# The last FFN product with token tiles stationary: two transformer layers in fp32 on one NeuronCore

## The chip, the cores and the metric

One core of a Trainium2 chip runs one launch of the kernel. The metric is the device time of that launch in microseconds (us), as the median of the runs; lower is better. Sequence length is 256, model width 2048, all inputs and outputs are fp32.

## The reference, cut to what matters

Two layers: multi-head latent attention and a convolutional FFN, then sliding-window attention and a second FFN, then a final norm. The change touches what follows the second FFN's gate:

```python
def _rmsnorm(x, g):
    y = xf * lax.rsqrt(jnp.mean(xf * xf, axis=-1, keepdims=True) + EPS)
    return (y * g.astype(F32)).astype(x.dtype)
...
    return (jax.nn.silu(gate) * val) @ w_out        # (256 x 5632) @ (5632 x 2048)
...
        h = h + _conv_ffn(_rmsnorm(h, norm_ffn[i]), ...)
    return _rmsnorm(h, final_norm)
```

## The kernel before, in words

**Weights in chunks.** All weights form one stream of 682 chunks of 128 x 1024 floats (512 KB). For the last product (phase `f1_out`, 88 chunks) a chunk holds two row tiles of 128 rows of `w_out` by 512 columns. Each chunk goes through four slots: SyncE loads it into `raw` (L364), ScalarE copies it to `w_hi` in the reduced format fp32r (`split`, L822), VectorE subtracts to get the rest `w_lo` (`split`, L1103), TensorE uses both. The activation is held in the same two parts, `op_ffn[:, tile, 0, :]` high and `op_ffn[:, tile, 1, :]` low, so that high by high, high by low and low by high give nearly fp32 products.

**The order of work** is written by hand in a block per engine and bound by semaphores. `lo_ready` counts chunks split, `chunk_used` chunks that TensorE has used. ScalarE's split of chunk n waits until chunk n-4 is used; SyncE's load waits for the split of the chunk that had the slot. The engines' other work is put between the splits.

**The last product** (`groups` with `w_chunk`, L419) has 4 groups of 22 chunks. A group makes 512 features for all 256 tokens, features on the partitions. Weights are stationary: for each of 4 feature tiles and 2 row tiles, `feature_tile` (L406) issues `w_hi` against high and low part of the activation side by side (512 moving columns, L409) and `w_lo` against the high part (256 moving columns, L412), so a chunk is 8 + 8 matmuls. In a group's last chunk the second row tile has the two in the other order. A group uses 4 of the 8 PSUM banks, and the groups alternate. VectorE adds the two halves of a bank to the residual `h` (features on partitions) in two passes (L1353, L1360), after the split of the third chunk beyond the group. GpSimd squares `h` of the first three groups and adds up (L1612, L1615). VectorE multiplies their 12 tiles by the final gain (L1377) between splits of the last group.

**The end.** After the last matmul of the last group: VectorE adds the last residual (L1353, L1360), TensorE transposes 16 tiles of 128 x 128 (L789), then 8, then sums squares over partitions with one-column matmuls (L803, L805), ScalarE squares the last 512 features (L1080), loads its table and takes the root (L1082), VectorE inverts it (L1591). TensorE transposes the last 8 tiles. ScalarE (L1088) and VectorE (L1596) scale the transposed tiles out of PSUM into `yt`, and SyncE stores four pieces of 512 KB (L397), each of 128 tokens by 1024 features, each after one pass of both engines.

Phases of attention have two other kinds of product that the prediction draws on: `token_chunk` (L430), where a tile of 128 tokens is stationary and 256 columns of the weights move (L438 to L440), and `narrow_chunk` (L691 to L693), where weights are stationary and 256 columns of the activation move, three times.

## Time and profile before

| | |
|---|---|
| median of 3 runs | 2021.43 us (2020.96 to 2022.01) |
| the profiled execution | 2018.73 us, its span 2016.7 us |
| TensorE busy, matmul | 1984.6 us (98%) |
| TensorE busy, weight load | 1763.1 us (87%) |
| VectorE busy | 1432.0 us (71%) |
| ScalarE busy | 987.3 us (49%) |
| GpSimd busy | 145.2 us (7%) |
| DMA | 374.46 MB, mean 186 GB/s |

The profile is of one execution. Its own time lies 2.0 us above its span, and 2.7 us below the median of the runs. "Busy" counts instructions that execute; matmuls overlap in the pipeline, so the distance from one start to the next says what a matmul costs, and its duration does not. "Idle before" is the time in which an engine waited in front of an instruction, with the releaser.

### The profile page before, as it was taken

The numbers are of one execution on the slowest core, as the hardware profiler recorded it, in microseconds if no ns is written. First come the engines' busy times: TensorE is split into PE (matmuls) and PEld (weight loads), VectorE is DVE, ScalarE is ACT, GpSimd is POOL, SyncE is SP. The second block draws the span as 40 slices with busy tenths as digits, with TensorE's granted clock in tenths as the row PEclk, the third lists the DMA queues.
The fourth block names the chain that finished last, engine by engine and source line by source line (L and its number), as shares of the span: only waits on it lengthen the run. The fifth ranks groups of instructions, "written<-read, shape, count | busy, mean of one in ns | idle before, by whom it ended". The sixth has DMA issues, their size and how long they took to land.

```text
span 2016.7 us, 33814 instructions
## 1 busy us (share of the span) xinstructions
PE 1984.6 (98%) x12008; PEld 1763.1 (87%) x12008; DVE 1432.0 (71%) x1980; ACT 987.3 (49%) x1151; POOL 145.2 (7%) x147
## 2 busy tenths in 40 slices
PE   7899999999999999999999999999999999999998
PEld 6798888888888888888899888888888888888887
DVE  7866777787788777555566668878887887855554
ACT  6456345555554554334445554555455555533332
POOL 1103230000000000110120004100000000001110
PEclk9999999999999999999999999999999999999999
DMA  7457555555555555555565334555556555555553
GB/s 277 151 195 167 178 188 186 199 189 182 198 185 175 196 194 195 185 188 198 188 236 185 126 127 161 199 193 187 177 189 206 188 179 196 186 195 190 189 188 115
DMA packets 103880, 374.46 MB, mean 186 GB/s; under 512 B 11547, under 2 KB 12124, under 8 KB 103548
## 3 DMA queue, kind: packets, MB, share of 16 engines
q1 hardware_dynamic: 101180, 362.55, 53.0%
q0 software_dynamic: 2624, 10.83, 2.1%
q8 instruction: 56, 0.92, 0.2%
q14 instruction: 20, 0.16, 0.0%
HBM read 364.94 MB, written 8.39 MB: 185 GB/s over the span
## 4 chain that ended last, share of the span: by engine, by line
PE 90%; DVE 5%; issue 1%; ACT 0%; DVEq 0%; ACTq 0%
PE ps L409 53%; PE ps L412 28%; PE ps L691 2%; PE ps L693 1%; PE ps L692 1%; DVE w_lo L1103 1%; DVE scores_b L1496 1%; PE ps L729 1%; PE ps L740 1%; PE ps L752 1%; PE ps L440 1%; PE ps L439 1%; PE ps L438 1%; DVE cv L1118 0%; PE ps L621 0%
## 5 line engine op out<-in xcount | busy, mean ns | idle before, releaser
L1103 DVE TENSOR_TENSOR w_lo<-raw,w_hi 128x1024 fp32r<-128x1024 f32 (+1 forms) x682 | 829.9, 1230 | 498.2 <-ACT w_hi L822 476.8
L822 ACT ACTIVATE w_hi<-raw 128x1024 fp32r<-128x1024 f32 (+1 forms) x682 | 715.2, 1055 | 794.6 <-PE ps L412 607.3
L409 PE MATMUL ps<-op_in,w_hi 128*128 128x512 f32 x2992 | 1028.0, 391 | 9.4 <-DVE w_lo L1103 9.4
L412 PE MATMUL ps<-op_in,w_lo 128*128 128x256 f32 x2992 | 812.9, 282 | 0.0
L409 PEld LDWEIGHTS ps<-op_in,w_hi 128*128 128x128 f32 x2992 | 549.6, 188 | 113.7 <-issue 8.3
L412 PEld LDWEIGHTS ps<-op_in,w_lo 128*128 128x128 f32 x2992 | 565.5, 189 | 15.7
L409 PE MATMUL ps<-op_ffn,w_hi 128*128 128x512 f32 x1408 | 486.2, 390 | 0.0
L412 PE MATMUL ps<-op_ffn,w_lo 128*128 128x256 f32 x1408 | 391.7, 282 | 0.0
L409 PEld LDWEIGHTS ps<-op_ffn,w_hi 128*128 128x128 f32 x1408 | 262.2, 188 | 53.0
L412 PEld LDWEIGHTS ps<-op_ffn,w_lo 128*128 128x128 f32 x1408 | 266.0, 189 | 2.7
L1612 POOL TENSOR_TENSOR cg<-h 128x1024 f32 (+1 forms) x15 | 43.1, 2876 | 1604.9 <-DVE h L1360 1454.4
L409 PE MATMUL ps<-op_att,w_hi 128*128 128x512 f32 x384 | 132.3, 392 | 2.7 <-issue 1.5
L412 PE MATMUL ps<-op_att,w_lo 128*128 128x256 f32 x384 | 104.2, 282 | 0.0
L409 PEld LDWEIGHTS ps<-op_att,w_hi 128*128 128x128 f32 x384 | 70.5, 188 | 16.5 <-issue 1.6
L1405 DVE SCALAR_TENSOR_TENSOR cv<-up,par,cv 128x256 f32<-128x256 f32 x176 | 73.6, 480 | 6.5 <-DVE cv L1400 3.4
L1405 DVE SCALAR_TENSOR_TENSOR cg<-up,par,cg 128x256 f32<-128x256 f32 x176 | 73.6, 480 | 6.6 <-DVE cg L1400 3.4
L412 PEld LDWEIGHTS ps<-op_att,w_lo 128*128 128x128 f32 x384 | 72.5, 189 | 1.9
L691 PE MATMUL ps<-op_in,w_hi 128*128 128x256 f32 x256 | 73.5, 287 | 0.0
L692 PE MATMUL ps<-op_in,w_lo 128*128 128x256 f32 x256 | 71.4, 279 | 0.0
L693 PE MATMUL ps<-op_in,w_hi 128*128 128x256 f32 x256 | 71.4, 279 | 0.0
L835 ACT ACTIVATE op_ffn<-cv 128x1024 f32 x22 | 23.4, 1066 | 93.0 <-DVE cv L1430 93.0
L1615 POOL TENSOR_TENSOR sqa<-sqa,cg 128x256 f32<-128x256 f32 x60 | 62.6, 1043 | 4.7
(198 smaller groups left out, 1626.2 us busy)
## 6 DMA issues: line engine op xcount, KB each, us to landing
raw<-weights SPq DMA_DIRECT2D x666, 512.0 KB, 3.8
raw<-weights SPq DMA_DIRECT2D x16, 384.0 KB, 3.1
bias_rows<-brow POOLq DMA_DIRECT2D x1, 6144.0 KB, 36.6
win_bias<-bias_rows POOLq DMA_DIRECT2D x4, 1024.0 KB, 8.4
h<-xt SPq DMA_DIRECT2D x8, 256.0 KB, 8.1
x_tok<-x_rows SPq DMA_DIRECT2D x2, 1024.0 KB, 10.6
y<-yt SPq DMA_DIRECT2D x4, 512.0 KB, 4.0
par<-params SPq DMA_DIRECT2D x1, 352.0 KB, 11.9
```

The source lines that it names most:

```text
L409: return mm(ps[:, bank, 0:2 * T], whi, op, start=start, stop=stop)
L412: return mm(ps[:, bank, 0:T], wlo, op[:, 0, :], start=False, stop=False)
L438: mm(o, hi, wcols(w_hi[s], k), start=first and k == 0, stop=False)
L691: mm(o, w_hi[s][:, w], op[:, kt0 + k, 0, :], start=first and k == 0 and j % 2 == 0, stop=False)
L692: mm(o, w_lo[s][:, w], op[:, kt0 + k, 0, :], start=False, stop=False)
L693: z = mm(o, w_hi[s][:, w], op[:, kt0 + k, 1, :], start=False, stop=last and k == 1 and j % 2 == 1)
L822: f(w_hi[s][:, 0:cols], raw[s][:, 0:cols], ACT.Copy).then_inc(hi_ready, 1)
L835: f(dst, cv[:, :, :], ACT.Copy).then_inc(operand_hi, 1)
L1103: v.tensor_tensor(w_lo[s][:, 0:cols], raw[s][:, 0:cols], w_hi[s][:, 0:cols].bitcast(F32), ALU.subtract).then_inc(lo_ready, 1)
L1405: z = v.scalar_tensor_tensor(dst[:, m, :], up[:, m, tap:T + tap], col(tile0 + (w + tap * CT + m)), dst[:, m, :], ALU.mult, ALU.add)
L1612: done(g_.tensor_tensor(tmp, src, src, ALU.mult))
L1615: z = g_.tensor_tensor(acc[:, :], acc[:, :], tmp[:, j, :], ALU.add)
```

## The change: what it does

- The last product is computed with tokens on the partitions. `rows_chunk` takes 128 tokens of the activation as the stationary operand (high part twice, low part once) and 512 columns of the chunk's weights as the moving one: for 2 token tiles and 2 row tiles `hi` by `w_hi`, `hi` by `w_lo`, `lo` by `w_hi`. That is 12 matmuls of 512 columns for a chunk. A group fills 2 banks.
- `turn_h`: after the ninth chunk of each group TensorE transposes the 8 tiles of the group's part of the old residual into the other 2 banks of the group's four, and ScalarE copies them back over `h`, 4 x 256 columns, which now holds tokens on the partitions.
- VectorE adds product and residual in two passes of 128 x 512 for each group (`add_rows`), multiplies by the gain, now a row (`gain_rows`), into `yt`. ScalarE squares each half and sums along the row (`accum_out`), and takes the root from the sum of the last group with the sum of the other three as bias; it has taken a root of that bias earlier in the last group.
- The rows of `gain_row` (1 MB, one row read for all partitions) come by a DMA of GpSimd after the last chunk of `f1_in`. GpSimd's squares for the final norm are gone; so are the end's transposes and one-column matmuls, and the gains by feature.
- `yt` is scaled in place and stored in eight pieces of 256 KB, 128 tokens by 512 features each.

```diff
...
     ra = region(KT * 2 * T * 4)
     op_in = place("op_in", [P, KT, 2, T], F32R, ra)
     yt = place("yt", [P, 2, D], F32, ra)
+    gain_row = place("gain_row", [P, D], F32, ra + 2 * D * 4)
     probs_t = [place("probs_t0", [P, 2, 384], F32, ra), place("probs_t1", [P, 2, 384], F32, ra + 29312)]
     scores_sb = place("scores_sb", [P, 2, 2, 384], F32, ra + 3072)
...
             rest = PH["a_kv"].c0
             repeat(sp, 0, (CHUNKS - rest) // SLOTS, lambda i: [load(Lin(rest + k, SLOTS, i)) for k in range(SLOTS)])
-            for k in range(4):
-                half, cols = k // 2, slice(k % 2 * (D // 2), (k % 2 + 1) * (D // 2))
-                sp.wait_ge(y_act, k + 1)
-                sp.wait_ge(y_dve, k + 1)
-                sp.dma_start(out[half * P:(half + 1) * P, cols], yt[:, half, cols]).then_inc(stored, 16)
-            sp.wait_ge(stored, 64)
+            for half in range(2):
+                for ready, q in ((y_act, 0), (y_dve, 2), (y_act, 1), (y_dve, 3)):
+                    sp.wait_ge(ready, 2 * half + q % 2 + 1)
+                    cols = slice(q * COLS, (q + 1) * COLS)
+                    sp.dma_start(out[half * P:(half + 1) * P, cols], yt[:, half, cols]).then_inc(stored, 16)
+            sp.wait_ge(stored, 128)
             sp.wait_ge(bias_out, 16)
...
                 for c in range(8):
                     w_chunk(Lin(ph.c0 + 8 * gi + c), op_att, 2 * c, c == 0, c == 7, b0).then_inc(chunk_used, 1)
             groups(PH["f1_in"], op_in, KT, op_wait(OP0["b_out"]), norm=5)
-            groups(PH["f1_out"], op_ffn, FT, op_wait(OP0["f1_in"]))
-
-
-            def transposes(q, src, bank):
-
-                pe.wait_ge(y_scaled, q + 1)
+
+            ph = PH["f1_out"]
+
+            def rows_chunk(n, kt0, first, last, bank):
+
+                s = n % SLOTS
+                pe.wait_ge(lo_ready, n + 1)
                 for half in range(2):
-                    if q == 3 and half == 1:
-                        pe.wait_ge(norm_root_taken, 7)
-                    for j in range(4):
-                        z = nc.tensor.transpose(ps[:, bank + half, j * P:(j + 1) * P],
-                                                src(j)[:, half * P:(half + 1) * P], ident[:, :])
-                    z.then_inc(y_transposed, 1)
-            yb = OUT_BANKS
-            pe.wait_ge(banks_free, PH["f1_out"].g1 - 1)
-            transposes(0, lambda j: h[:, j, :], yb[0])
-            transposes(1, lambda j: h[:, 4 + j, :], yb[1])
-            pe.wait_ge(banks_free, PH["f1_out"].g1)
-            transposes(2, lambda j: h[:, 8 + j, :], yb[2])
-            pe.wait_ge(squares_added, NORM_SQ[6])
-            pe.wait_ge(last_squares, 1)
-            for half in range(2):
-                tokens = slice(half * P, (half + 1) * P)
-                o = ps[:, yb[3] + 1, half:half + 1]
-                mm(o, sqa[:, tokens], ones[:, 0:1], start=True, stop=False)
+                    t = slice(half * P, (half + 1) * P)
+                    for k in range(2):
+                        w = slice(k * COLS, (k + 1) * COLS)
+                        hi, lo = op_ffn[:, kt0 + k, 0, t], op_ffn[:, kt0 + k, 1, t]
+                        mm(ps[:, bank + half, :], hi, w_hi[s][:, w], start=first and k == 0, stop=False)
+                        mm(ps[:, bank + half, :], hi, w_lo[s][:, w], start=False, stop=False)
+                        z = mm(ps[:, bank + half, :], lo, w_hi[s][:, w], start=False, stop=last and k == 1)
+                z.then_inc(chunk_used, 1)
+
+            def turn_h(g, bank):
+
+                if g >= 2:
+                    pe.wait_ge(h_turned, g - 1)
                 for j in range(4):
-                    z = mm(o, cg[:, j, tokens], ones[:, 0:1], start=False, stop=j == 3)
-            z.then_inc(norm_sum, 1)
-            transposes(3, lambda j: cv[:, j, :], yb[3])
+                    for half in range(2):
+                        at = j % 2 * T + half * P
+                        z = nc.tensor.transpose(ps[:, bank + j // 2, at:at + P],
+                                                h[:, 4 * g + j, half * P:(half + 1) * P], ident[:, :])
+                z.then_inc(h_transposed, 1)
+            for g in range(4):
+                b0 = 4 * (g % 2)
+                if g < 2:
+                    pe.wait_ge(banks_free, ph.g0 + g - 1)
+                else:
+                    pe.wait_ge(y_summed, 2 * (g - 1))
+                for c in range(FT // 2):
+                    if g == 0 and c % 2 == 0:
+                        pe.wait_ge(operand_lo, OP0["f1_in"] + c // 2 + 1)
+                    rows_chunk(ph.c0 + FT // 2 * g + c, 2 * c, c == 0, c == FT // 2 - 1, b0)
+                    if c == 8:
+                        turn_h(g, b0 + 2)
         @block.scalar
...
             residual(PH["b_out"], KT, OP0["b_out"], second=True)
             norm_root(5, inv_rms[:, :], 4 - 4 * (PH["f1_in"].g0 % 2), D)
             ffn_in(PH["f1_in"], 1, OP0["f1_in"])
-            residual(PH["f1_out"], FT, None)
-
-
-            act.wait_ge(banks_free, PH["f1_out"].g1)
-            f(cg[:, :, :], h[:, KT - 4:KT, :], ACT.Square).then_inc(last_squares, 1)
-            act.wait_ge(norm_sum, 7)
-            f(rs_col[:, 4:6], ps[:, OUT_BANKS[3] + 1, 0:2], ACT.Sqrt, bias=eps[:, 0:1],
-              scale=1.0 / D).then_inc(norm_root_taken, 1)
-            act.wait_ge(sqrt_done, 1)
+
+            ph = PH["f1_out"]
+
+            def quads(bank):
+
+                a = ps[:, bank, 0:T]
+                return bass.AP(a.tensor, a.offset, [list(a.ap[0]), [T, 4], [1, T]])
+            for g in range(4):
+                for c in range(FT // 2):
+                    split(Lin(ph.c0 + AHEAD + FT // 2 * g + c))
+                    if c == 6:
+                        act.wait_ge(h_transposed, g + 1)
+                        f(h[:, 4 * g:4 * g + 4, :], quads(4 * (g % 2) + 2), ACT.Copy).then_inc(h_turned, 1)
+                    if c == 19:
+                        for half in range(2):
+                            act.wait_ge(y_summed, 2 * g + half + 1)
+                            f(cg[:, 0:4, half * P:(half + 1) * P], h[:, 4 * g:4 * g + 4, half * P:(half + 1) * P],
+                              ACT.Square, scale=D ** -0.5,
+                              accum_out=y_sums[:, g, half:half + 1]).then_inc(y_squared, 1)
+                            if g == 3:
+                                act.wait_ge(y_squared, 7 + half)
+                                f(y_rs[:, half:half + 1], y_sums[:, 3, half:half + 1], ACT.Sqrt,
+                                  bias=y_rest[:, half:half + 1]).then_inc(norm_root_taken, 1)
+                    if g == 3 and c == 4:
+                        act.wait_ge(y_rest_ready, 1)
+                        f(y_rs[:, :], y_rest[:, :], ACT.Sqrt)
             for half in range(2):
-                for q in (0, 2):
-                    act.wait_ge(y_transposed, 2 * q + half + 1)
-                    f(yt[:, half, q * 512:(q + 1) * 512], ps[:, OUT_BANKS[q] + half, :], ACT.Copy,
-                      scale=rs_col[:, 4 + half:5 + half]).then_inc(y_act, 1)
+                act.wait_ge(y_rs_ready, half + 1)
+                for q in range(2):
+                    cols = slice(q * COLS, (q + 1) * COLS)
+                    f(yt[:, half, cols], yt[:, half, cols], ACT.Copy, scale=y_rs[:, half:half + 1]).then_inc(y_act, 1)
         @block.vector
...
             inverse(5, [inv_rms[:, :]])
             dve.wait_ge(operand_lo, OP0["b_out"] + 4)
             ffn_in(PH["f1_in"], 1, OP0["f1_in"])
-            residual(PH["f1_out"], FT, None, None, static=True)
-
-
-            for m in range(4):
-                z = v.tensor_scalar(cv[:, m, :], h[:, KT - 4 + m, :], col(Lin(PC_FIN + KT - 4 + m)), None, ALU.mult)
-            z.then_inc(y_scaled, 1)
-            dve.wait_ge(norm_root_taken, 7)
-            v.reciprocal(rs_col[:, 4:6], rs_col[:, 4:6]).then_inc(sqrt_done, 1)
-            dve.wait_ge(sqrt_done, 1)
+
+            ph = PH["f1_out"]
+
+            def rows(g, half):
+                return h[:, 4 * g:4 * g + 4, half * P:(half + 1) * P]
+
+            def add_rows(g, half):
+
+                o = ps[:, 4 * (g % 2) + half, :].rearrange("p (m t) -> p m t", m=4)
+                v.tensor_tensor(rows(g, half), o, rows(g, half), ALU.add).then_inc(y_summed, 1)
+
+            def gain_rows(g, half):
+
+                cols = slice(g * COLS, (g + 1) * COLS)
+                dve.wait_ge(y_summed, 2 * g + half + 1)
+                v.tensor_tensor(yt[:, half, cols].rearrange("p (m t) -> p m t", m=4), rows(g, half),
+                                gain_row[:, cols].rearrange("p (m t) -> p m t", m=4), ALU.mult).then_inc(y_gained, 1)
+
+            def inverse_rms(half):
+
+                dve.wait_ge(norm_root_taken, 7 + half)
+                v.reciprocal(y_rs[:, half:half + 1], y_rs[:, half:half + 1]).then_inc(y_rs_ready, 1)
+            for g in range(4):
+                for c in range(FT // 2):
+                    split(Lin(ph.c0 + AHEAD + FT // 2 * g + c))
+                    if c == 17:
+                        dve.wait_ge(h_turned, g + 1)
+                        dve.wait_ge(chunk_used, ph.c0 + FT // 2 * (g + 1))
+                        add_rows(g, 0)
+                        add_rows(g, 1)
+                    if c == 19 and g < 3:
+                        if g == 0:
+                            dve.wait_ge(gain_row_in, 16)
+                        gain_rows(g, 0)
+                        gain_rows(g, 1)
+                    if g == 3 and c == 2:
+                        dve.wait_ge(y_squared, 6)
+                        done(v.tensor_tensor(y_rest[:, :], y_sums[:, 0, :], y_sums[:, 1, :], ALU.add))
+                        done.sync()
+                        done(v.tensor_tensor(y_rest[:, :], y_rest[:, :], y_sums[:, 2, :], ALU.add))
+                        done.sync()
+                        v.tensor_scalar(y_rest[:, :], y_rest[:, :], EPS, None, ALU.add).then_inc(y_rest_ready, 1)
+            gain_rows(3, 0)
+            inverse_rms(0)
+            gain_rows(3, 1)
+            inverse_rms(1)
+            dve.wait_ge(y_gained, 8)
             for half in range(2):
-                for q in (1, 3):
-                    dve.wait_ge(y_transposed, 2 * q + half + 1)
-                    v.tensor_scalar(yt[:, half, q * 512:(q + 1) * 512], ps[:, OUT_BANKS[q] + half, :],
-                                    rs_col[:, 4 + half:5 + half], None, ALU.mult).then_inc(y_dve, 1)
+                dve.wait_ge(y_rs_ready, half + 1)
+                for q in range(2, 4):
+                    cols = slice(q * COLS, (q + 1) * COLS)
+                    v.tensor_scalar(yt[:, half, cols], yt[:, half, cols], y_rs[:, half:half + 1], None,
+                                    ALU.mult).then_inc(y_dve, 1)
         @block.gpsimd
...
                 heads = bass.AP(bias_dram.tensor, P - 1 + 8 * k * P * 384, [[383, P], [P * 384, 8], [1, T]])
                 pool.dma_start(win_bias[:, 8 * k:8 * k + 8, :], heads).then_inc(win_bias_in[k], 16)
             residual_squares(PH["b_out"], SQ0["b_out"])
-            pool.wait_ge(norm_sum, 6)
-            done(g_.memset(sqa[:, :], 0.0))
-            done.sync()
-            for gi in range(3):
-                pool.wait_ge(banks_free, PH["f1_out"].g0 + gi + 1)
-                squares(h[:, 4 * gi:4 * gi + 4, :], cg[:, :, :], sqa, None)
-                pool.wait_ge(squares_added, SQ0["f1_out"] + gi + 1)
+            pool.wait_ge(chunk_used, PH["f1_in"].c1)
+            pool.dma_start(gain_row[:, :], bass.AP(final_gain.tensor, 0, [[0, P], [1, D]])).then_inc(gain_row_in, 16)
 def tables():
```

TensorE in the last product before, where one chunk ends and the next begins (all chunks of a group but its last look so). The names are PSUM, then the moving operand, then the stationary one.

```order
L412 MATMUL ps<-op_ffn,w_lo_58 128x256
L409 MATMUL ps<-op_ffn,w_hi_54 128x512
L412 MATMUL ps<-op_ffn,w_lo_58 128x256
L409 MATMUL ps<-op_ffn,w_hi_55 128x512 [waits lo_ready]
L412 MATMUL ps<-op_ffn,w_lo_59 128x256
```

A pair of 512 and 256 columns alternates, eight times for each chunk, with one wait at a chunk's start. The same place of the second group now, around the transposes (`ident` moves, a tile of `h` is stationary):

```order
L798 MATMUL ps<-w_hi_53,op_ffn 128x512
L796 MATMUL ps<-w_hi_53,op_ffn 128x512
L797 MATMUL ps<-w_lo_57,op_ffn 128x512
L798 MATMUL ps<-w_hi_53,op_ffn 128x512
L808 MATMUL ps<-ident,h 128x128 x8
L796 MATMUL ps<-w_hi_54,op_ffn 128x512 [waits lo_ready]
L797 MATMUL ps<-w_lo_58,op_ffn 128x512
L798 MATMUL ps<-w_hi_54,op_ffn 128x512
```

All matmuls have 512 columns, and the eight transposes wait for nothing here (in the third and fourth group the first of them waits for `h_turned`).

VectorE's program after its last split, before:

```order
L1353 TENSOR_TENSOR h<-h,ps 128x1024 [waits banks_free,chunk_used]
L1360 TENSOR_TENSOR h<-h,ps 128x1024 [waits dve_done]
L1588 TENSOR_SCALAR cv<-h,par 128x256 [waits banks_free]
L1588 TENSOR_SCALAR cv<-h,par 128x256 x3
L1591 RECIPROCAL rs_col<-rs_col 128x2 [waits norm_root_taken]
L1596 TENSOR_SCALAR yt<-ps,rs_col 128x512 [waits y_transposed,sqrt_done]
L1596 TENSOR_SCALAR yt<-ps,rs_col 128x512 [waits y_transposed] x3
```

and now:

```order
L1612 TENSOR_TENSOR h<-ps,h 128x4x128 [waits chunk_used,h_turned]
L1612 TENSOR_TENSOR h<-ps,h 128x4x128
L1618 TENSOR_TENSOR yt<-h,gain_row 128x512 [waits y_summed]
L1624 RECIPROCAL y_rs<-y_rs 128x1 [waits norm_root_taken]
L1618 TENSOR_TENSOR yt<-h,gain_row 128x512 [waits y_summed]
L1624 RECIPROCAL y_rs<-y_rs 128x1 [waits norm_root_taken]
L1654 TENSOR_SCALAR yt<-yt,y_rs 128x512 [waits y_rs_ready,y_gained]
```

The passes are half as wide, nothing waits for TensorE after the first row, and each half of the tokens has its own root. ScalarE's end, now:

```order
L1104 ACTIVATE cg,y_sums<-h 128x4x128 [waits y_summed]
L1109 ACTIVATE y_rs<-y_sums,y_rest 128x1 [waits y_squared]
L1104 ACTIVATE cg,y_sums<-h 128x4x128 [waits y_summed]
L1109 ACTIVATE y_rs<-y_sums,y_rest 128x1 [waits y_squared]
L1118 ACTIVATE yt<-yt,y_rs 128x512 [waits y_rs_ready]
```

Both roots stand ahead of the first scaled copy, and no table is loaded there.

## Rows read from the trace of the kernel before

**Rows 1.** The page: granted clock by slice, and the chain's shares by engine.

```profile
PEclk9999999999999999999999999999999999999999
...
PE 90%; DVE 5%; issue 1%; ACT 0%; DVEq 0%; ACTq 0%
```

**Rows 2.** Waits, 1758 to 2001 us: who waited for whom, us, times, longest.

```profile
ACT w_hi L822 <- PE ps L412: 132.7, 78, 2.0
DVE w_lo L1103 <- ACT w_hi L822: 107.1, 76, 1.8
```

**Rows 3.** Timeline, ScalarE: start us, us, engine, line, out<-in, [idle before <-releaser].

```profile
1824.20 1.06 ACT L822 ACTIVATE w_hi<-raw 128x1024 fp32r<-128x1024 f32 x1 [1.71 <-PE ps L412]
...
1871.34 1.06 ACT L822 ACTIVATE w_hi<-raw 128x1024 fp32r<-128x1024 f32 x1 [1.71 <-PE ps L412]
```

**Rows 4.** Timeline, TensorE, last chunk of the last group (order turned round).

```profile
1998.92 0.40 PE L412 MATMUL ps<-op_ffn,w_lo 128*128 128x256 f32 x2
...
2001.01 0.40 PE L412 MATMUL ps<-op_ffn,w_lo 128*128 128x256 f32 x2
2001.25 0.39 PE L409 MATMUL ps<-op_ffn,w_hi 128*128 128x512 f32 x1
```

**Rows 5.** Timeline, TensorE, 256 columns of the activation moving.

```profile
1042.35 0.28 PE L691 MATMUL ps<-op_in,w_hi 128*128 128x256 f32 x1
...
1055.65 0.28 PE L691 MATMUL ps<-op_in,w_hi 128*128 128x256 f32 x1
```

**Rows 6.** Timeline, TensorE, 256 columns of the weights moving.

```profile
1038.11 0.28 PE L438 MATMUL ps<-w_hi,op_in 128*128 128x256 f32 x1
...
1039.53 0.39 PE L409 MATMUL ps<-op_in,w_hi 128*128 128x512 f32 x1
```

**Rows 7.** Timeline, ScalarE: splits released by a group's last matmul.

```profile
1291.20 1.06 ACT L822 ACTIVATE w_hi<-raw 128x1024 fp32r<-128x1024 f32 x1 [1.71 <-PE ps L409]
...
1757.54 1.06 ACT L822 ACTIVATE w_hi<-raw 128x1024 fp32r<-128x1024 f32 x1 [1.72 <-PE ps L409]
```

**Rows 8.** Timeline, TensorE, six transposes among an attention phase's matmuls.

```profile
1097.40 0.28 PE L693 MATMUL ps<-op_in,w_hi 128*128 128x256 f32 x1
1097.82 0.84 PE L740 MATMUL ps<-ident,probs_b 128*128 128x128 f32 x6
1098.42 0.37 PE L691 MATMUL ps<-op_in,w_hi 128*128 128x256 f32 x1
1098.62 0.28 PE L692 MATMUL ps<-op_in,w_lo 128*128 128x256 f32 x1
```

**Rows 9.** Timeline, all engines, the end.

```profile
2001.48 1.91 PE L789 MATMUL ps<-ident,h 128*128 128x128 f32 x16
2001.68 1.22 DVE L1353 TENSOR_TENSOR h<-h,ps 128x1024 f32<-128x1024 f32 x1 [8.72 <-PE ps L409]
...
2004.19 1.06 ACT L1080 ACTIVATE cg<-h 128x1024 f32<-128x1024 f32 x1 [12.49 <-DVE h L1360]
...
2007.79 0.26 ACT L1082 ACTIVATE rs_col<-ps,eps 128x2 f32<-128x2 f32 x1 [1.25 <-PE ps L805]
...
2009.14 2.95 SPq L397 DMA_DIRECT2D y<-yt  x4
```

**Rows 10.** Groups by line and shape: xcount | busy us, mean ns | idle before.

```profile
L1246 DVE TENSOR_TENSOR q_nope<-ps,half_b 128x512 f32<-128x512 f32 x4 | 2.7, 685 | 0.0
...
L1088 ACT ACTIVATE yt<-ps,rs_col 128x512 f32<-128x512 f32 x4 | 2.4, 688 | 0.2 <-PE ps L789 0.2
...
L789 PE MATMUL ps<-ident,h 128*128 128x128 f32 x24 | 3.0, 275 | 0.8 <-DVE h L1360 0.8
```

**Rows 11.** DMA: packets of 2010 to 2015 us (the stores), then of the first 20 us.

```profile
DMA packets 539, 2.02 MB, mean 403 GB/s; under 512 B 48, under 2 KB 48, under 8 KB 538
...
DMA packets 2471, 6.53 MB, mean 327 GB/s; under 512 B 265, under 2 KB 521, under 8 KB 2347
```

**Rows 12.** Waits, 1042 to 1056 us, with 1 MB loads of GpSimd under way.

```profile
ACT w_hi L822 <- DMA raw<-weights: 3.6, 2, 1.9
```

More of the change, by code:

```diff
@@ L95, in attention_banks @@
     return scores, 4 - scores, 6 - scores
-OUT_BANKS = [(4 * (PH["f1_out"].g1 % 2) + 2 * k) % 8 for k in range(4)]
 class Lin:
@@ L343, in build @@
         outputs_lo = sem("outputs_lo")
-        y_scaled = sem("y_scaled")
-        last_squares = sem("last_squares")
-        y_transposed = sem("y_transposed")
+        gain_row_in = sem("gain_row_in")
+        h_transposed = sem("h_transposed")
+        h_turned = sem("h_turned")
+        y_summed = sem("y_summed")
+        y_squared = sem("y_squared")
+        y_gained = sem("y_gained")
+        y_rs_ready = sem("y_rs_ready")
+        y_rest_ready = sem("y_rest_ready")
         y_act = sem("y_act")
@@ L981, in residual @@
                     body(None, 1)
-                elif k0 is not None:
+                else:
                     repeat(act, 0, 2, body)
-                else:
-                    body(None, 0)
-                    body(None, 1)
             def ffn_in(ph, layer, k0):
@@ L1389, in residual @@
                     body(None, 1)
-                elif static:
-                    for t in range(turns):
-                        body(None, t)
                 else:
```

19 lines of the change are left out of this document (8 added, 11 removed).

## The prediction

> **What bounds the kernel now.** I read the page first: the chain that ended last is 90% TensorE, and the granted clock is at its upper level, 2.4 GHz, in every slice [rows 1]. Then the waits of the last product's stretch: ScalarE waits for TensorE 78 times, VectorE for ScalarE 76 times, and no row has TensorE waiting [rows 2]. So in this stretch a weight chunk costs what TensorE takes to issue its matmuls. From 1824.20 to 1871.34 us there are 17 chunks, 47.14 / 17 = 2.773 us each [rows 3]; 88 chunks make 244.0 us. Behind the last matmul the end is a chain through all engines: VectorE starts at 2001.68, the first store is issued at 2009.14 [rows 9], and the span ends at 2016.7. That is 7.46 us to the first store, 7.6 us from there, and 15.05 us in all. A faster matmul stream and a shorter end both count in full; all that hides behind TensorE counts nothing.
>
> All sums are against the profiled execution, 2018.73 us. The median of the runs lies 2.7 us above it, and I add that at the end. A measurement can tell about 0.2% (4 us) from no change.
>
> **Term 1, the matmuls.** Removed are 16 a chunk, 8 of 512 and 8 of 256 moving columns, added are 12 of 512: 6144 columns either way. The question is what a 512-column matmul costs when only such follow each other, and when weights move. A pair of 512 and 256 now costs 2.773 / 8 = 0.3466 us. Alone, 256 columns of the activation cost (1055.65 - 1042.35) / 38 / 3 = 0.1167 us [rows 5], which leaves 0.2299 for the 512. The last chunk of a group has 512 behind 512: from 1998.92 to 2001.01 there are three sets of two and two, 0.6967 each [rows 4]. Less one pair, that is 0.3501 for one 256 behind a 256 and one 512 behind a 512. With 0.40 - 0.28 = 0.12 for the first of these [rows 4] the 512 costs 0.230, with 0.1167 it costs 0.2334. I take the middle, 0.232, which also leaves something for the weights as moving operand: 12 matmuls with 256 columns of weights took 1039.53 - 1038.11 = 1.42 us, 0.1183 each [rows 6] against 0.1167. A chunk is then 12 x 0.232 = 2.784 us, 0.011 more than now, and 88 of them cost **+1.0 us**.
>
> The bounds. Most: 21 groups of 8 chunks took 1757.54 - 1291.20 = 466.34 us [rows 7], 22.207 each, or 0.023 above 8 x 2.773. If all of that is the four 512-behind-512 of a group's end, each costs 0.2299 + 0.0058 = 0.2357, and +4.9 us in all. Least: a 256 behind another is 0.12 in rows 4 and 0.1167 in a long run of them [rows 5], so equal neighbours may get cheaper in a run; the same 0.0033 off 0.2301 leaves 0.2268, and -4.5 us. One nanosecond per matmul is 1.06 us here, and nothing else in the sum weighs as much.
>
> **Term 2, the transposes in the stream.** Each group now has 8. Six of them among the attention's matmuls start at 1097.82 and the next matmul starts at 1098.42, 0.100 each, and that one costs 0.20 instead of 0.117, so 0.083 for the change back [rows 8]. The 16 behind the last product took 1.91 - 0.27 = 1.64 us for 15 steps, 0.109 each [rows 9], where 0.27 is the length of one [rows 10]. So a group pays 8 x 0.109 + 0.08 = 0.95 us, four pay **+3.8 us**. At least it is 4 x 0.8 = 3.2. At most the gap ahead of the six also counts, 0.42 - 0.12 = 0.30 us [rows 8], which makes 5.0; but the 16 started 0.23 us behind the last 512-column matmul [rows 4, 9], with no such gap. Of the waits for `h_turned` in groups 2 and 3, ScalarE's copy is two groups old, so I cost them at nothing.
>
> What that transposing feeds costs nothing either: ScalarE's copy of 1024 columns (about the 1.06 of its split) and VectorE's passes for three groups go into the idle time of engines that wait 1.7 us in each chunk of 2.77 [rows 3]. The adds stand where the old ones stood. If this cover were gone, each us would go straight to TensorE through `lo_ready`.
>
> **Term 3, the end.** Counted from VectorE's start, 0.43 us behind the last matmul's start [rows 4, 9], which I keep. One add of 128x512: 0.69 [rows 10]. ScalarE's square of half the tokens: 0.65, between half of L1080's 1.06 [rows 9] and the 0.69 of a pass of 512 out of PSUM [rows 10], and 0.10 for reading the sum, an estimate of mine below the root's 0.26, the smallest pass of ScalarE in the rows. Together 0.75. Root 0.26 [rows 9]. The second square and root come before the first scaled copy: another 1.01. The copy 0.69 [rows 10]. Sum 0.69 + 0.75 + 0.26 + 1.01 + 0.69 = 3.40, with four handovers of 0.035 (2004.19 is 2.51 behind 2001.68, with two passes of 1.22 between [rows 9]) 3.55 us to the first store, instead of 7.46. VectorE meanwhile needs four passes of 0.69, 2.8, and two reciprocals of two columns, and is not late. What is late next is the DMA. The stores are 2.10 MB at 403 GB/s, 5.2 us [rows 11], out of the 7.6 behind the first issue, and smaller pieces do not shorten that: a piece of 256 KB takes 0.65 us, and two engines finish one each 0.3. So 3.55 + 7.6 = 11.15 instead of 15.05, **-3.9 us**. Bounds: pieces with rows of 2 KB may go at the 327 GB/s of the mixed loads at the start [rows 11], 1.2 us more, and a late copy may add 0.4: -2.3. Squares at half of L1080, 0.53 without a tail: -4.3, rounded to -4.5.
>
> **Term 4, edits that cost nothing.** The 1 MB of gains lands beside the first chunks. In the attention phase such loads made ScalarE wait 3.6 us for `raw` [rows 12], while VectorE and TensorE went on. GpSimd's squares and VectorE's gains were behind TensorE and give nothing back.
>
> **Sum.** 1.0 + 3.8 - 3.9 = +0.9 us: 2019.6 for a profiled execution, **2022.3 us** as a median. The extremes are -4.5 + 3.2 - 4.5 = -5.8 and +4.9 + 5.0 - 2.3 = +7.6. The work that leaves the end goes into the stream at nearly the same price.
>
> **Rivals.**
> - *Cheaper matmuls (faster).* With a fixed 10 ns beside the columns, as at 256 (0.1167 against 256 / 2.4 GHz = 0.1067), a 512 costs 0.2233, a chunk 2.680, and the total is -8.2 + 3.8 - 3.9 = -8.3: 2013.1. For it: fewer instructions and weight loads. Against: the pairs leave 0.2299. Chance 0.09. A further step is a matmul at its bare columns, 512 / 2.4 GHz = 0.2133: 12 of them make 2.560, the term is -18.7 and the total -18.8, 2002.6. No row here comes near it. Chance 0.03.
>  The Trainium skill ("TensorE: Matmul & The Clock Gate", section "Wait — 56ns, not 53.3ns?") gives 215.7 ns from start to start at 512 columns once warm, close to that last case; by it the term would be -16.1 us. The trace disagrees, with 0.2299 in the pairs.
> - *Weights moving are dear (slower).* At 0.2357 for each matmul of L796 to L798, from the groups' ends, the total is +4.9 + 3.8 - 3.9 = +4.8: 2026.2. It decides above 0.2350. For it: rows 6, where moving weights cost 1.6 ns more, which may double at 512. Against: the group's end may hold its own wait. Chance 0.14.
> - *Each transpose costs its length (slower).* At 0.275 us each [rows 10] the 32 would cost 8.8 + 0.3, and the total is 1.0 + 9.1 - 3.9 = +6.2: 2027.6. Against: 16 of them took 1.91 us [rows 9]. Chance 0.04.
>  The Trainium skill (same page, "Part 4: PE-mode transpose") has about 275 ns for one in a kernel, and speaks against this change; the trace has that as the length, 0.27, and 0.109 as the distance.
> - *The end does not get shorter as said:* the stores bound it from the first issue, and with -2.3 instead of -3.9 the total is +2.5, 2023.9, still no change that can be told. It is part of my case.
>
> **How the numbers follow.** My case, all terms within their bounds and the total within 4 us: 0.67, centre 2022.3, its own range 2018.5 to 2025.4. Faster: 0.12 from the matmuls and 0.02 from all bounds falling low, 0.14. Slower: 0.14 + 0.04 + 0.01 for a wait that I have not seen, 0.19. The range reaches down to about the lower extreme, 2016.0, and up to the dear cases, 2027.5; outside are the fast matmuls and the far end of the transposes.
>
> **What would show it.** ScalarE's splits 2.784 us apart in the last product (2.68 or 2.83 for two rivals); 8 transposes within 0.95 us, with no idle of TensorE ahead of them; first store 3.5 us behind VectorE's add, and the span's end 11.2 behind it; no TensorE waits from 1758 on. If VectorE or ScalarE is named as releaser of TensorE there, or `raw` in the first ten chunks, my cover is wrong.

## The result, and the profile after

| | before | after |
|---|---|---|
| median of 20 runs, us | 2021.1 (2018.15 to 2022.84) | 2025.3 (2022.48 to 2026.21) |
| ratio, 95% interval | | 1.0019 [1.0013, 1.0026] |
| profiled execution, us | 2018.73, span 2016.7 | 2025.74, span 2023.9 |

One run of 2179.81 us, at a granted clock of 0.849, is left out of the range and of the ratio; the other 19 have a median of 2025.0. The change makes the kernel some 4 us slower, just under the 0.2% from which a difference counts here; the forecast was +0.9 us, 2022.3.

The page of the kernel after: busy times, granted clock in 40 slices of 50 us, the chain's shares by engine.

```profile
PE 1987.8 (98%) x11636; PEld 1738.0 (86%) x11636; DVE 1423.3 (70%) x1976; ACT 995.7 (49%) x1172; POOL 122.7 (6%) x132
PEclk9999999999999999999999999999999999999999
PE 92%; DVE 3%; issue 1%; ACT 0%; ACTq 0%; DVEq 0%
```

The waits of the changed product, 1758 to 2024 us (who waited for whom: us, times, longest).

```profile
ACT w_hi L837 <- PE ps L798: 132.8, 81, 2.6
DVE w_lo L1132 <- ACT w_hi L837: 122.9, 82, 2.5
ACT cg L1104 <- DVE h L1612: 10.9, 1, 10.9
DVE h L1612 <- PE ps L798: 8.9, 1, 8.9
```

As in [rows 2], TensorE waits for nobody there. One group's transposes, in the timelines of ScalarE (first four rows) and of TensorE: start us, us, engine, line, operation, out<-in, [idle before <-releaser].

```profile
1847.69 1.06 ACT L837 ACTIVATE w_hi<-raw 128x1024 fp32r<-128x1024 f32 x1 [1.74 <-PE ps L798]
1850.48 1.06 ACT L837 ACTIVATE w_hi<-raw 128x1024 fp32r<-128x1024 f32 x1 [1.73 <-PE ps L798]
1854.16 1.06 ACT L837 ACTIVATE w_hi<-raw 128x1024 fp32r<-128x1024 f32 x1 [2.62 <-PE ps L798]
1856.96 1.06 ACT L837 ACTIVATE w_hi<-raw 128x1024 fp32r<-128x1024 f32 x1 [1.74 <-PE ps L798]
...
1849.99 0.39 PE L798 MATMUL ps<-w_hi,op_ffn 128*128 128x512 f32 x1
1850.22 1.04 PE L808 MATMUL ps<-ident,h 128*128 128x128 f32 x8
1851.02 0.48 PE L796 MATMUL ps<-w_hi,op_ffn 128*128 128x512 f32 x1
1851.34 0.40 PE L797 MATMUL ps<-w_lo,op_ffn 128*128 128x512 f32 x1
1851.57 0.40 PE L798 MATMUL ps<-w_hi,op_ffn 128*128 128x512 f32 x1
...
1857.17 0.40 PE L798 MATMUL ps<-w_hi,op_ffn 128*128 128x512 f32 x1
```

A chunk takes 2.80 us (1856.96 less 1854.16) instead of 2.773 [rows 3], and from 1851.57 to 1857.17 there are 24 matmuls of 512 columns, 0.2333 each. The chunk with the transposes takes 3.68, 0.88 more: the eight lie 0.100 apart (1851.02 less 1850.22), and the first matmul behind them takes 0.32 instead of 0.233.

The end, where [rows 9] was, as the timeline has it: the last matmul, the passes of VectorE and ScalarE, the stores.

```profile
2012.21 0.40 PE L798 MATMUL ps<-w_hi,op_ffn 128*128 128x512 f32 x1
2012.72 1.29 DVE L1612 TENSOR_TENSOR h<-ps,h 128x512 f32<-128x512 f32 x2 [8.89 <-PE ps L798]
2013.44 0.63 ACT L1104 ACTIVATE cg<-h 128x512 f32<-128x512 f32 x1 [10.87 <-DVE h L1612]
2013.98 0.19 ACT L1104 ACTIVATION_READ_ACCUMULATOR cg<-h 128x1 f32 x1
2014.20 0.29 ACT L1109 ACTIVATE y_rs<-y_sums,y_rest 128x1 f32<-128x1 f32 x1
2014.40 0.61 ACT L1104 ACTIVATE cg<-h 128x512 f32<-128x512 f32 x1
2015.14 0.29 ACT L1109 ACTIVATE y_rs<-y_sums,y_rest 128x1 f32<-128x1 f32 x1
2015.34 2.54 ACT L1118 ACTIVATE yt<-yt,y_rs 128x512 f32<-128x512 f32 x4
2015.56 1.67 DVE L1654 TENSOR_SCALAR yt<-yt,y_rs 128x512 f32<-128x512 f32 x4
2016.07 4.48 SPq L402 DMA_DIRECT2D y<-yt  x8
```

The first store is issued 3.35 us behind VectorE's start instead of 7.46, and the span's end, 2023.9, is 11.69 us behind the start of the last matmul instead of 15.45 (2016.7 less 2001.25, [rows 4]).

**Where the difference lies.** I cut both records at one mark: ScalarE's split beside the last group end of the product before the last. It is at 1757.54 before [rows 7], and in the timeline of after at:

```profile
1295.99 1.06 ACT L837 ACTIVATE w_hi<-raw 128x1024 fp32r<-128x1024 f32 x1 [1.74 <-PE ps L414]
...
1762.75 1.06 ACT L837 ACTIVATE w_hi<-raw 128x1024 fp32r<-128x1024 f32 x1 [1.74 <-PE ps L414]
```

| stretch, us | before | after | difference |
|---|---|---|---|
| start to the mark | 1757.54 | 1762.75 | +5.2 |
| mark to the last matmul's start | 243.71 | 249.46 | +5.75 |
| last matmul's start to the span's end | 15.45 | 11.69 | -3.76 |

What I had costed, the last two rows, comes to +2.0 us. The other 5.2 us arise before the first instruction that the change was meant to touch. The same two rows of after show a part of it: 21 groups in 466.76 us, 22.227 each, where [rows 7] have 22.207. So the experiments had two tasks: the split of the +2.0, and the cause of the rest.

### The profile page after: what moved, and what is told of

It is laid out like the page before. It is cut to its first block, busy times and chain, and to the rows that moved or that the text cites. A ratio compares the mean times of both kernels' runs of the same rounds, so it can differ in the third digit from the quotient of the medians.

```text
span 2023.9 us, 33059 instructions
## 1 busy us (share of the span) xinstructions
PE 1987.8 (98%) x11636; PEld 1738.0 (86%) x11636; DVE 1423.3 (70%) x1976; ACT 995.7 (49%) x1172; POOL 122.7 (6%) x132
## 4 chain that ended last, share of the span: by engine, by line
PE 92%; DVE 3%; issue 1%; ACT 0%; ACTq 0%; DVEq 0%
PE ps L414 46%; PE ps L417 23%; PE ps L798 4%; PE ps L797 4%; PE ps L796 4%; PE ps L696 2%; PE ps L697 2%; PE ps L698 2%; DVE w_lo L1132 1%; PE ps L734 1%; PE ps L745 1%; PE ps L757 1%; PE ps L444 1%; PE ps L443 1%; PE ps L445 1%
## 5 line engine op out<-in xcount | busy, mean ns | idle before, releaser
L417 PE MATMUL ps<-op_in,w_lo 128*128 128x256 f32 x2992 | 807.4, 280 | 0.0
L414 PE MATMUL ps<-op_ffn,w_hi 128*128 128x512 f32 x704 | 243.2, 392 | 0.0
L417 PE MATMUL ps<-op_ffn,w_lo 128*128 128x256 f32 x704 | 194.2, 280 | 0.0
L414 PEld LDWEIGHTS ps<-op_ffn,w_hi 128*128 128x128 f32 x704 | 131.1, 188 | 27.9
L798 PE MATMUL ps<-w_hi,op_ffn 128*128 128x512 f32 x352 | 140.4, 399 | 0.0
L797 PE MATMUL ps<-w_lo,op_ffn 128*128 128x512 f32 x352 | 138.7, 394 | 0.0
L796 PE MATMUL ps<-w_hi,op_ffn 128*128 128x512 f32 x352 | 138.4, 393 | 0.0
L417 PEld LDWEIGHTS ps<-op_ffn,w_lo 128*128 128x128 f32 x704 | 132.2, 188 | 1.4
L1670 POOL TENSOR_TENSOR cg<-h 128x1024 f32 x12 | 34.6, 2880 | 960.0 <-DVE h L1389 808.8
L797 PEld LDWEIGHTS ps<-w_lo,op_ffn 128*128 128x128 f32 x352 | 66.1, 188 | 17.0
L796 PEld LDWEIGHTS ps<-w_hi,op_ffn 128*128 128x128 f32 x352 | 66.1, 188 | 15.5
L798 PEld LDWEIGHTS ps<-w_hi,op_ffn 128*128 128x128 f32 x352 | 66.1, 188 | 15.3
```

The source lines that it names most:

```text
L414: return mm(ps[:, bank, 0:2 * T], whi, op, start=start, stop=stop)
L417: return mm(ps[:, bank, 0:T], wlo, op[:, 0, :], start=False, stop=False)
L796: mm(ps[:, bank + half, :], hi, w_hi[s][:, w], start=first and k == 0, stop=False)
L797: mm(ps[:, bank + half, :], hi, w_lo[s][:, w], start=False, stop=False)
L798: z = mm(ps[:, bank + half, :], lo, w_hi[s][:, w], start=False, stop=last and k == 1)
L1670: done(g_.tensor_tensor(tmp, src, src, ALU.mult))
```

## The experiments

### Three small tensors: put into the kernel before, and taken out of the new one

The change also adds `y_sums`, `y_rest` and `y_rs`, 32 bytes a partition each. The region with `op_in` and `op_ffn` comes behind them, and its start is rounded up to a multiple of 128 bytes plus 32; 96 bytes more push it 128 bytes up.

```diff
+    pad = new("pad", [P, 24])
     exp_sums = new(...)
```

> The kernel before with 96 bytes of unused SBUF where the change puts its three small tensors, so that all later tiles (op_in, op_ffn among them) lie 128 bytes higher, as in the changed kernel. Theory A (the addresses cost): the splits behind a group of f1_in come 22.227 us apart as in the changed kernel, not 22.207 as before, and the time is 2 us above before (ratio 1.001). Theory B (it was the execution, not the program): 22.207 and a ratio of 1.000.

And the new kernel with the three tensors laid over `sinkc`, which is not needed by then:

```diff
-    y_sums = new("y_sums", [P, 4, 2])
-    y_rest = new("y_rest", [P, 2])
-    y_rs = new("y_rs", [P, 2])
-    sinkc = new("sinkc", [P, HEADS_B])
+    r_sinkc = region(HEADS_B * 4)
+    sinkc = place("sinkc", [P, HEADS_B], F32, r_sinkc)
+    y_sums = place("y_sums", [P, 4, 2], F32, r_sinkc)
+    y_rest = place("y_rest", [P, 2], F32, r_sinkc + 32)
+    y_rs = place("y_rs", [P, 2], F32, r_sinkc + 64)
```

> The changed kernel with its three small tensors laid over sinkc, which is dead by then, so that nothing else moves. Theory A: 22.207 us between the groups of f1_in, ratio to before 1.001 (the 2.0 us that the last product and the end cost together). Theory B: as the changed kernel, 1.002.

The pad alone: 2023.4 us (11 runs) against 2020.66 (27), ratio 1.0017 [1.0008, 1.0026]. The new kernel without the shift: 2022.2 (11 runs), 1.0011 [1.0002, 1.0020]. (The ratios here are those on record; the quotients of the medians, 1.0014 and 1.0008, lie within the intervals.) The two marks in the timeline of the padded kernel, then of the new one without the shift:

```profile
1293.95 1.06 ACT L823 ACTIVATE w_hi<-raw 128x1024 fp32r<-128x1024 f32 x1 [1.74 <-PE ps L410]
1760.71 1.06 ACT L823 ACTIVATE w_hi<-raw 128x1024 fp32r<-128x1024 f32 x1 [1.74 <-PE ps L410]
```

```profile
1290.86 1.06 ACT L838 ACTIVATE w_hi<-raw 128x1024 fp32r<-128x1024 f32 x1 [1.72 <-PE ps L415]
1757.19 1.06 ACT L838 ACTIVATE w_hi<-raw 128x1024 fp32r<-128x1024 f32 x1 [1.72 <-PE ps L415]
```

That is 466.76 us with the pad, to the digit what the new kernel takes, and 466.33 without the shift, against 466.34 before. 96 bytes that nobody reads cost the kernel some 3 us, and only the addresses of the tensors behind them can do it: the instructions are the same. Within a group the chunks keep their 2.77; what grows is the last one, from 2.78 to 2.80 (1762.75 is 2.80 behind the split before it). From the mark on the kernel without the shift takes 249.46 us to the last matmul, the same as the new one, so the local +2.0 does not depend on it.

The groups are not the whole of it. From ScalarE's split at about 64 us on, the padded kernel falls behind the kernel before by 0.38 us up to the group end at 219.38, by 0.58 more up to 1019.12, by 1.16 up to 1246.40, and by 0.46 up to the mark, 2.58 in all. The largest part lies in the stretch with the second attention: 227.28 us before and 227.30 without the shift, 228.44 with the pad and 228.46 in a second record of the new kernel. No run here says why.

### Without the transposes

```diff
-                    if c == 8:
-                        turn_h(g, b0 + 2)
...
-                    if c == 6:
-                        act.wait_ge(h_transposed, g + 1)
-                        f(h[:, 4 * g:4 * g + 4, :], quads(...), ACT.Copy).then_inc(h_turned, 1)
...
-                        dve.wait_ge(h_turned, g + 1)
```

> The changed kernel without the 32 transposes of the residual and without ScalarE's four copies of them, so the residual is added in the wrong layout. Theory (transposes in the stream cost what the trace shows): 3.4 us less than the changed kernel, ratio to before 1.0002. Rival (the transposes fill time that TensorE would lose anyway): less than 1 us gained, ratio 1.0015 or more.

2021.25 us (11 runs), ratio to before 1.0005 [0.9996, 1.0014], which is 2.8 us below the new kernel's 1.0019. The mark is at 1761.66 and the last matmul at 2007.63: 245.97 us, 3.49 less than with the transposes, 0.87 a group. The chunks stay at 2.80. So what is left over the 243.71 of before, 2.26 us, I put down to the matmuls.

### Are the matmuls dear by their addresses?

The region of the weights 32 bytes on, so that `w_hi` lies at 32 of 128 (its address modulo 128) and the operands, unchanged, also at 32:

```diff
+    region(32)
     w_hi = [new(f"w_hi{s}", ...
```

> The changed kernel with w_hi, w_lo and the tiles up to the operands 32 bytes higher, the operand regions where they were. Theory C (512 moving columns of weights cost 0.2333 us for their address, the operands being laid 32 bytes off a multiple of 128): the matmuls of L797 come down to about 0.230, a chunk from 2.80 to 2.76 us, ratio to before 1.0003. Rival D (it is the run of wide matmuls, not the address): 2.80 stays, ratio 1.0019.

Then, from the kernel without the shift, the operands at 64 of 128 with the weights at 0, and both edits together:

```diff
-    top[0] = (top[0] + 127) // 128 * 128 + 32
+    top[0] = (top[0] + 127) // 128 * 128 + 64
```

> As e2_after_noshift, but the operand regions (op_in, op_ffn and what shares them) start 64 bytes beyond a multiple of 128 instead of 32, the weights at a multiple of 128. Only the distances in the trace are read. Theory R (what counts is where stationary and moving operand lie to each other): both kinds of chunk change. Theory M (what counts is where the moving operand lies): the old kind (operand moves) changes from 2.773 us, the new kind (weights move) stays at 2.800. Theory N (addresses below 128 bytes don't matter): both stay.

> Weights 32 bytes and operand regions 64 bytes beyond a multiple of 128, so that the two lie to each other as before. Theory R: old chunks 2.773, new ones 2.800. Theory M: new ones 2.79 as with the weights at 32 and the operands at 32, old ones as in e5_op64. Theory N: fails already on the run with the weights at 32, where old chunks took 2.81.

| weights, operands (address modulo 128) | a group of the old kind, us | mark to last matmul in the new product, us |
|---|---|---|
| 0, 32 (before for the groups; without the shift) | 22.207 | 249.46 |
| 0, 32, operands 128 bytes up (after; pad for the groups) | 22.227 | 249.46 |
| 32, 64 | 22.227 | 249.46 |
| 0, 64 | 22.327 | 249.47 |
| 32, 32 | 22.453 | 248.69 |

The two dearest are means of the last 20 groups. In the row 32, 64 the rounding also puts the operands 128 bytes further up, if the weights of before start at a multiple of 128 as the table has it; it then differs from the second row by 32 bytes on both sides, and has the same times. The times of the whole kernel went the same way: 2038.2 us for weights and operands both at 32 (4 runs, ratio 1.0092 [1.0077, 1.0108]), and in a single run each 2030.8 for 0 and 64, 2024.8 for 32 and 64. In the first of these the old chunks take 2.81 us each; splits of the old kind and then of the new one, in its timeline:

```profile
1314.67 1.07 ACT L838 ACTIVATE w_hi<-raw 128x1024 fp32r<-128x1024 f32 x1 [1.75 <-PE ps L418]
1317.48 1.07 ACT L838 ACTIVATE w_hi<-raw 128x1024 fp32r<-128x1024 f32 x1 [1.74 <-PE ps L418]
...
1896.91 1.06 ACT L838 ACTIVATE w_hi<-raw 128x1024 fp32r<-128x1024 f32 x1 [1.72 <-PE ps L799]
1899.70 1.06 ACT L838 ACTIVATE w_hi<-raw 128x1024 fp32r<-128x1024 f32 x1 [1.73 <-PE ps L799]
```

For the question of the new chunk this was a miss: its 2.80 us hold at four of the five placements and fall only to 2.79 at the fifth (248.69 less 249.46 is 0.77 us over 88 chunks, 0.7 ns a matmul). At the addresses of the new kernel the 512-column matmul costs 0.2333, not the 0.232 that I had taken, and none of these moves is worth more than that 0.7 ns. For the rest of the kernel it was a find: the old kind of chunk is cheapest with a distance of 32 bytes between the residues, dearer with 64, dearest with 0. That is a pattern over five placements, each of which moves other tensors too, and its cause was not looked for.

### The same transposing on VectorE

The kernel without the shift, with the residual turned in blocks of 32x32 by VectorE into `cv`, which is free then: two instructions behind each weight split, 16 steps a group. TensorE's transposes and ScalarE's copies are gone.

```diff
-                        turn_h(g, b0 + 2)
-                        f(h[:, 4 * g:4 * g + 4, :], quads(...), ACT.Copy).then_inc(h_turned, 1)
-                v.tensor_tensor(rows(g, half), o, rows(g, half), ALU.add)
+                v.tensor_tensor(rows(g, half), o, cv[:, 0:4, half * P:(half + 1) * P], ALU.add)
+            def turn_block(g, k):
+                a, b = divmod(k, 4)
+                for half in range(2):
+                    src = h[32 * a:32 * a + 32, 4 * g:4 * g + 4, half * P + 32 * b:half * P + 32 * b + 32]
+                    dst = cv[32 * b:32 * b + 32, 0:4, half * P + 32 * a:half * P + 32 * a + 32]
+                    z = v.transpose(dst, src)
+                z.then_inc(h_turned, 1)
```

> e2_after_noshift with the residual transposed by VectorE instead of TensorE: 16 steps a group, each of two 32 x 512-element blocks of 32x32 transposes that also go to another quarter of the partitions, one step behind each of the first 16 splits; TensorE's 32 transposes and ScalarE's four copies are gone. Theory (VectorE waits 1.5 us in each chunk of 2.8, so steps of about 0.5 us hide): 3.4 us less than e2, ratio to before 0.9993, 1.4 us faster than before. Rival (VectorE becomes late with w_lo, since its steps are far longer than 0.5 us): TensorE waits for VectorE, ratio above 1.001.

2019.4 us (11 runs, 2016.6 to 2021.6) against 2021.1 (21), ratio 0.9989 [0.9980, 0.9998]: the one version that beats both kernels, if by less than the 0.2% that counts here. VectorE in its timeline, and the waits from 1763 to 2015 us:

```profile
1849.85 1.22 DVE L1128 TENSOR_TENSOR w_lo<-raw,w_hi 128x1024 fp32r<-128x1024 f32 x1 [1.05 <-ACT w_hi L836]
1851.11 0.49 DVE L1616 STREAM_TRANSPOSE cv<-h 32x128 f32<-32x128 f32 x2
1852.65 1.22 DVE L1128 TENSOR_TENSOR w_lo<-raw,w_hi 128x1024 fp32r<-128x1024 f32 x1 [1.05 <-ACT w_hi L836]
```

```profile
ACT w_hi L836 <- PE ps L799: 134.1, 81, 2.0
DVE w_lo L1128 <- ACT w_hi L836: 83.0, 78, 1.6
```

The two block transposes take 0.49 us out of VectorE's idle 1.5 a chunk, and TensorE still waits for nobody. From the mark (1759.09) to the last matmul (2005.07) it is 245.98 us, as without any transposing. Its own sum against before is +2.27 - 3.7 = -1.4 us.

### Four stores of 512 KB in place of eight

```diff
-                for ready, q in ((y_act, 0), (y_dve, 2), (y_act, 1), (y_dve, 3)):
-                    sp.wait_ge(ready, 2 * half + q % 2 + 1)
-                    cols = slice(q * COLS, (q + 1) * COLS)
+                for ready, q in ((y_act, 0), (y_dve, 2)):
+                    sp.wait_ge(ready, 2 * half + 2)
+                    cols = slice(q * COLS, (q + 2) * COLS)
```

> e2_after_noshift with four stores of 512 KB (128 tokens by 1024 features, rows of 4 KB) instead of eight of 256 KB. Theory (the stores are bound by bandwidth, rows of 2 KB cost about 0.4 us of it, and the first store goes out 0.6 us later): within 0.4 us of e2, ratio to before 1.0011. Rival (small stores are what shortens the end): 1.5 us slower than e2, 1.0018.

2022.8 us (11 runs), 1.0008 [0.9999, 1.0018], within the spread of the 1.0011 with eight. The end in its timeline:

```profile
2008.92 0.40 PE L799 MATMUL ps<-w_hi,op_ffn 128*128 128x512 f32 x1
2013.39 2.89 SPq L403 DMA_DIRECT2D y<-yt  x4
```

The first store leaves 4.47 us behind the last matmul's start instead of 3.86, and the span ends 7.61 us after it (2021.0) instead of 7.83: 12.08 in all instead of 11.69. The smaller pieces are worth 0.4 us of the 3.8; their first issue is earlier by 0.6, and the stretch behind it gives 0.2 of that back, for the shorter rows or the larger number of stores, which this run does not separate.

### The rest before the mark: both kernels again, unchanged

In an untouched phase the granted clock falls to 0.50, in the first record of before at 66 to 70 us, in that of after at 75 to 79. The page's slices of 50 us hide it: they show 9 throughout.

> The kernel before, unchanged. In the records so far the granted clock falls to 0.50 once, either at 66 to 71 us (before and three of the variants) or at 74 to 79 us (the changed kernel and three of the variants), and the road from the weight split at 63.4 us to the one at 120.7 us then takes 57.2 to 57.5 or 59.4 to 59.5 us. Theory X, the place is drawn anew in every execution: both places, or 58.7 with a mixed one, can show up here, and the program's time moves with it by some 2 us. Theory Y, the place belongs to the program (its layout of the code or of the tensors): this program shows 66 to 71 us and 57.2 again, in both runs.

> The same once more. X: over the two pairs (before twice, changed twice) at least one differs from the first record of its program. Y: 57.2 us here.

> The changed kernel, unchanged. X: the fall of the clock lies at either place, and a record with it at 66 to 71 us spans some 2 us less than the 2023.9 us of the first. Y: at 74 to 79 us again, and 59.5 us from the split at 63.8 us to the one at 123.3 us, in both runs. Both: 249.5 us from the last group end of the input product to the last matmul, and 22.227 us for a group of eight chunks before it.

> The same once more. X: either place. Y: 74 to 79 us, 59.5 us. Both: 249.5 us and 22.227 us as above.

The times were 2020.6 and 2021.3 us (before), 2024.1 and 2024.9 (after). Windows of 2 us: the stretch, its length, then busy us of TensorE, of its weight loads, of VectorE, ScalarE and GpSimd with their counts, the granted clock, the DMA share and GB/s. First the first record of before, then the kernel before again, then the changed kernel again, twice:

```profile
64.00:66.00 2.00, 0.64 (x2) 0.14 (x2) 1.97 (x3) 1.35 (x3) 0.00 (x0) 1.00 0.91 250
66.00:68.00 2.00, 2.00 (x7) 1.62 (x7) 1.97 (x3) 0.48 (x1) 1.33 (x1) 0.53 0.36 143
68.00:70.00 2.00, 2.00 (x9) 1.76 (x8) 2.00 (x1) 0.00 (x0) 1.92 (x2) 0.62 0.57 195
```

```profile
64.00:66.00 2.00, 0.77 (x3) 0.18 (x3) 1.97 (x2) 1.22 (x3) 0.00 (x0) 1.00 0.86 255
66.00:68.00 2.00, 2.00 (x12) 1.79 (x12) 1.97 (x3) 0.48 (x1) 1.47 (x1) 1.00 0.37 138
...
72.00:74.00 2.00, 0.00 (x0) 0.00 (x0) 2.00 (x3) 0.03 (x1) 1.92 (x2) 1.00 0.53 187
74.00:76.00 2.00, 1.93 (x9) 1.73 (x10) 1.64 (x5) 0.00 (x0) 0.88 (x3) 0.87 0.77 247
76.00:78.00 2.00, 2.00 (x7) 1.71 (x7) 0.00 (x0) 0.01 (x1) 0.18 (x1) 0.50 0.48 146
```

```profile
64.00:66.00 2.00, 0.00 (x0) 0.00 (x0) 2.00 (x3) 2.00 (x3) 0.00 (x0) 1.00 0.31 106
66.00:68.00 2.00, 1.58 (x4) 0.66 (x5) 1.93 (x3) 0.90 (x3) 0.28 (x1) 0.72 0.78 263
68.00:70.00 2.00, 2.00 (x8) 1.71 (x7) 2.00 (x2) 0.00 (x0) 2.00 (x1) 0.50 0.23 83
```

```profile
68.00:70.00 2.00, 2.00 (x7) 1.65 (x7) 2.00 (x1) 0.09 (x1) 1.92 (x2) 0.50 0.52 187
...
90.00:92.00 2.00, 0.49 (x1) 0.50 (x2) 1.74 (x5) 1.31 (x2) 0.00 (x0) 0.81 0.53 192
92.00:94.00 2.00, 2.00 (x7) 1.63 (x7) 1.88 (x4) 0.00 (x0) 0.00 (x0) 0.50 0.01 5
```

So each program shows both places. Each fall comes right behind a pause of TensorE, the one at 64 us or the one at 72, and goes to 0.50, the lower level of 1.2 GHz; where it falls late, it had stayed at 1.00 behind the first pause. Which of the two it is changes from execution to execution. In the last record the clock falls early and then once more, behind a third pause, at 91 to 95 us. Of all 14 records of this case five have the early fall alone, six the late one, and three the early one and this second one. From ScalarE's split at about 63.5 us (64.47 in the third run) to the mark:

| fall of the clock | before | after | pad | without the shift |
|---|---|---|---|---|
| early | 1694.13 | 1696.70 | 1696.71 | 1694.09 |
| early, and again at 91 us | | 1698.15 | | |
| late | 1696.15, 1696.12 | 1698.95 | | 1696.12 (four stores), 1696.23 (transposing on VectorE) |

Read across, after against before, the table gives what the shift costs: 2.6 us early, 2.8 late. Read down, it gives what the late fall costs more than the early one: 2.0 to 2.3 us. TensorE's wait for GpSimd's `sqb` shows why, in the first record of before and then in that of after:

```profile
73.64 0.70 PE L452 MATMUL ps<-sqb,ones 128*128 128x256 f32 x2 [1.10 <-POOL sqb L1615]
```

```profile
74.60 0.86 PE L457 MATMUL ps<-sqb,ones 128*128 128x256 f32 x2 [2.44 <-POOL sqb L1673]
```

With the early fall the slow matmuls lie ahead of this wait and disappear in it, and 1.10 us of waiting are left over. With the late fall TensorE waits 2.44 us, GpSimd's last four passes take 4.82 us instead of 4.24, and the slow matmuls come behind the wait, where nothing hides them. This is read from the order of the instructions; no run changed it. My first records were one with the early fall before and one with the late fall after, and 2.3 of their 5.2 us are that draw. The last 0.4 of the 5.2 are the time up to 63.5 us (63.41 before, 63.80 after), which varies too, from 63.27 to 63.98 in before alone.

## Why the prediction was right, and where it was wrong

The forecast was 2022.3 us, the measured median 2025.3: inside the range, and at the upper end of my own case, 2018.5 to 2025.4. The direction and the signs of the three terms held; one term was missing. That the number still fell inside is in part luck: the sum would have missed a dear placement just as it missed this one, and with weights and operands both at 32 the same kernel took 2038.2 us, far outside. With the local +2.0 and 2.6 for the shift the records give +4.6 us; measured is a ratio of 1.0019, +3.8 us, [+2.6, +5.3].

- **Term 1, the matmuls: +2.3 us, forecast +1.0.** This is the term that was mis-sized. I had two readings of a 512 behind a 512, 0.230 and 0.2334, and took their middle, 0.232; the second was right (0.2333). It came from rows 4 with the 0.1167 of a long run of 256-column matmuls [rows 5] for the 256 behind a 256. The middle had no reason but caution. The bounds, 0.2268 and 0.2357, held it, and the rule stated there, 1.06 us a nanosecond, gives the difference. The dear rival, from 0.2350 on, did not come true. Nor did the cheap ones: the Trainium skill ("TensorE: Matmul & The Clock Gate", section "Wait — 56ns, not 53.3ns?") has 215.7 ns, and no record here, at any of five placements, comes below 0.2326, the mean with weights and operands at 32. (By the skill's figure the term is an estimated -16.2 us, where I had written -16.1.)
- **Term 2, the transposes: +3.5 us, forecast +3.8.** They lie 0.100 apart as in the attention [rows 8], not 0.109 as in the 16 of the old end [rows 9], and the handing back costs 0.09. No gap ahead of them. The rival of 0.275 each is out. The waits for `h_turned` cost nothing: none has TensorE behind it.
- **Term 3, the end: -3.76 us, forecast -3.9.** The first store 3.35 behind VectorE instead of 3.55: the squares took 0.54 before their sum was read where I had 0.65, and reading took 0.2 where I had 0.10. Behind it 7.83 instead of 7.6; four stores with longer rows took 7.61. VectorE starts 0.51 behind the last matmul's start instead of 0.43.
- **Term 4, the edits at nothing.** ScalarE waits once for `raw`, 2.2 us up to 1782.83, which it does not do before, and TensorE waits for nobody behind it. The gains had landed 12 us earlier (issued at 1763.0, 7.7 us), and whether their load is the cause was not tested. For the edits that I named this was right. It failed on one that I did not name: three tensors of 32 bytes. Their passes cost nothing, their place cost 2.6 us all over the program. The step that failed is the sentence that my sum has four terms: I priced every instruction that the change adds or moves, and no address.
- **The profile of one execution.** I had put the median 2.7 us above the first record and left it open why. The runs give a part of the answer: that record has the early fall of the clock. I had also read the granted clock as at its upper level in every slice; in windows of 2 us it is not, and a slice of 50 us does not show that.

What stays open: why 128 bytes at the same residue lengthen a group's last chunk by 0.02 us, and the stretch with the second attention by 1.2; what draws the place at which the clock falls; whether the pauses at 64 and 72 us can be closed, which was not tried.

## What to carry to other kernels

Moving work from a serial end into a stream that is bound by TensorE pays only for what goes to another engine: here 3.8 us of the end came back as 3.5 us of transposes and 2.3 us of matmuls, and with the transposes in VectorE's idle time, and without the shift, it became a gain, of 0.1%. Count the bytes that a change allocates as well as its instructions, and compare the marks of untouched phases before you explain the changed one: a difference that is there before the change begins is another cause. And before a difference of 0.2% between two records is explained, take each record again.
